# Reordering the end and the start of a scan unit: two masks ahead of the state's update, the first level between the masks, the state product inside the output products

## Chip, core and metric

The kernel runs on one core of one Trainium2 chip. The metric is device time in microseconds (us) of one execution. All arithmetic is fp32.

## What is computed

The reference is a two-layer network on 512 tokens of width 1024 (256 of context, 256 latent). Layer 0 mixes the tokens with a delta-rule scan (RWKV-7) and a diagonal scan, layer 1 with differential attention, and each layer ends in a table of 16384 experts of which every token gathers 128. The change lies in the delta-rule scan alone. It runs forwards and backwards over 8 heads of 64:

```python
def step(state, inp):
    r_t, w_t, k_t, v_t, kk_t, akk_t = inp
    sa = jnp.einsum('bhvk,bhk->bhv', state, kk_t)
    state = (state * w_t[:, :, None, :] - sa[..., None] * akk_t[:, :, None, :]
             + v_t[..., None] * k_t[:, :, None, :])
    return state, jnp.einsum('bhvk,bhk->bhv', state, r_t)
```

## The kernel before

`rwkv_scan` (L620) replaces the 512 steps by blocks of 128 tokens. A *unit* is one block in one direction. There are 8 (`UNITS`, L629), forwards and backwards in turn, and they run one after the other. Inside a unit every head needs four 128 x 128 products of its operands (the *scores*), masked to a triangle, and the inverse of a unit triangular matrix. Lines are those of the kernel before.

- **Scores (`scores`, L744, matmul at L747).** The scores of `bF` with `qrF` go to PSUM banks 6, 7, 4, 5 (`AE_BANKS`), those of `kF` with `qrF` to banks 0 to 3 (`BF_BANKS`). A call makes one pair of heads. Pairs 0 and 1 fill banks 6 and 7 (or 0 and 1), pairs 2 and 3 fill 4 and 5 (or 2 and 3).
- **Masks (L1019).** VectorE multiplies each of these eight banks by the triangle `seen` and writes `NE` (from the bF scores) or `BF` (from the kF scores), four instructions each, counted by the semaphore `seen_done`.
- **Levels.** The inverse `T` is built by doubling, `LEVELS` = 7. Level 0 transposes `NE` on TensorE (L805), and VectorE writes the result into the identity under a mask (L1030). Levels 1 to 5, for each group `g` of four heads, multiply `NE` by `T` (L803) and transpose `T` (L809), ScalarE evicts both (L918, L925), TensorE multiplies the two (L817) and VectorE merges the result into `T` (L1034). Level 6 is a half-sized form of it (L800, L819, L1036).
- **BV product (L783).** `BF` times the values, at the start of level 1, evicted by ScalarE (L906) into `qb`.
- **End of a unit.** L825 makes `W` and `U` from the inverse, evicted by ScalarE (L928) and VectorE (L1045). L834 makes the read-out's factor (bank 2, VectorE L1048). L838 to L840 make the state's transition `GT` and increment `H` (banks 4 and 5), which VectorE evicts in L1051, L1053 and two halves of L1056. L847 is the *state product* `GT` times `S0` (bank 0), to which L1062 adds `H` and which L1063 scales (`s_done`). L853, L855 and L857 are the *output products*, six instructions for each pair of heads, accumulated in bank 1 and evicted by L1067 or L1069 (`o_done`).
- **Preparation of the next unit.** It stands amid the levels: `lora` (L715) in level 1, `sums` (L723) in level 3, and `turn` (L730, L741) in levels 4 to 6, each with its part on ScalarE. GpSimd computes the operands between them (`prepare`, L936 to L974).

Every engine has its instructions in one order, written out by hand, and waits on semaphores. Nothing else sets the order. On TensorE an instruction that waits holds all behind it. In the order before, VectorE first waits until the output products of the unit have ended (L1013), then evicts NE's four masks, BF's four masks, and level 0. TensorE makes all scores, waits for NE's four masks, transposes, and waits for BF's four masks.

Of the kernel before, what the change touches and what calls it, by code (L numbers as in the profile page):

```python
# [18 lines left out]
P = 128  # L19
# [600 lines left out]
def rwkv_scan(nc, a, ident, low, rkv, kk, O, KT, rows_out):  # L620
# [13 lines left out]
    with Phase(nc) as ph:  # L634
# [27 lines left out]
        NE = ph.sb("NE", [P, HEADS, 2, P])  # L662
# [34 lines left out]
        with nc.Block() as block:  # L697
# [10 lines left out]
            def _(pe):  # L708
# [55 lines left out]
                for n, (d, t) in enumerate(UNITS):  # L764
                    b = n % 2
                    if n == 0:
                        scores_ae(n, 0)
                        scores_ae(n, 1)
# [3 lines left out]
                    scores_ae(n, 3)  # L772
                    if n >= 1:
                        pe.wait_ge(s_done, n)
                        pe.wait_ge(r_done, n)
                        pe.wait_ge(o_done, n)
                    for pair in range(4):
                        scores(n, kF, BF_BANKS, bf_mm, pair)
                    for lv in range(LEVELS):
# [5 lines left out]
                        for g in range(2):  # L785

                            if g == 1 and n + 1 < NU:
                                if lv == LORA_AT:
                                    lora(n + 1)
                                if lv == SUMS_AT:  # L790
                                    sums(n + 1)
                                if lv in TURN_AT:
                                    turn(n + 1, TURN_AT[lv])
                            if lv:
                                pe.wait_ge(y_done, 2 * (LEVELS * n + lv - 1) + g + 1)
                            else:
                                pe.wait_ge(seen_done, 8 * n + 4)
                            for h in range(4 * g, 4 * g + 4):
                                if lv == LEVELS - 1:
                                    m = nc.tensor.matmul(ps[into[d], g, cols(h)], NE[from_[d], h, 0, into[d]], T[from_[d], h, from_[d]],  # L800
                                                         start=True, stop=True)
                                elif lv:
                                    m = nc.tensor.matmul(ps[:, g, (h % 4) * P:(h % 4) * P + P], NE[:, h, 0], T[:, h], start=True, stop=True)  # L803
                                else:
                                    m = nc.tensor.transpose(ps[:, 4 + g, (h % 4) * P:(h % 4) * P + P], NE[:, h, 0], ident[:])  # L805
                            m.then_inc(x_mm, 1)
                            if lv:
                                for h in range(4 * g, 4 * g + 4):
                                    m = nc.tensor.transpose(ps[:, 4 + g, (h % 4) * P:(h % 4) * P + P], T[:, h], ident[:])  # L809
                                m.then_inc(tt_mm, 1)  # L810
                        if lv:
                            for g in range(2):
                                pe.wait_ge(x_done, 2 * ((LEVELS - 1) * n + lv - 1) + g + 1)
                                pe.wait_ge(tt_done, 2 * ((LEVELS - 1) * n + lv - 1) + g + 1)
                                for h in range(4 * g, 4 * g + 4):
                                    if lv < LEVELS - 1:
                                        m = nc.tensor.matmul(ps[:, 2 + g, (h % 4) * P:(h % 4) * P + P], TT[:, h], X[:, h], start=True, stop=True)  # L817
                                    else:
                                        m = nc.tensor.matmul(ps[from_[d], 2 + g, cols(h)], X[into[d], h, 0:HD], TT[into[d], h, into[d]],  # L819
                                                             start=True, stop=True)  # L820
                                m.then_inc(y_mm, 1)
# [39 lines left out]
            def _(act):  # L861
# [42 lines left out]
                for n, (d, t) in enumerate(UNITS):  # L904
                    act.wait_ge(bv_mm, n + 1)
                    nc.scalar.activation(qb[:, n % 2, :, 1], ps[:, 6].rearrange("p (h d) -> p h d", h=HEADS), ACT.Copy).then_inc(bv_done, 1)  # L906
                    for lv in range(LEVELS):
                        for g in range(2 if lv else 0):
                            if g == 1 and n + 1 < NU:
                                if lv == LORA_AT:  # L910
                                    lora(n + 1)
# [8 lines left out]
                            else:  # L920
# [5 lines left out]
                                                 ACT.Copy).then_inc(tt_done, 1)  # L926
# [1177 lines left out]
```

## Time and profile before

| | |
|---|---|
| Time, median of 3 runs | 3215.91 us (3214.31 to 3221.04) |
| The profiled execution's own time | 3196.97 us |
| Its span | 3195.2 us |
| The scan's units, 8 of them | from about 318 us to 750 us of the span |
| A unit in the steady part | about 54.6 us |
| TensorE busy over the span | 2642.8 us (83%) |
| VectorE busy over the span | 2107.6 us (66%) |

The profiled execution is one run with the hardware profiler on, and it is not one of the three. A row of the timeline gives start, length, engine, line, operation, output and inputs, shape and count; in square brackets stands how long the engine was idle before it and what released it. Consecutive instructions of one line are merged. An fp32 matmul of 8 heads or tiles shows as 16 entries, a transpose as one each. TensorE's lengths reach past the start of the next row, because matmuls are pipelined: the distance from start to start is what a row costs while the engine is fed.

### The profile page before, as it was taken

The numbers are of one execution on the slowest core, as the hardware profiler recorded it, in microseconds if no ns is written. First come the engines' busy times: TensorE is split into PE (matmuls) and PEld (weight loads), VectorE is DVE, ScalarE is ACT, GpSimd is POOL, SyncE is SP. The second block draws the span as 40 slices with busy tenths as digits, with TensorE's granted clock in tenths as the row PEclk, the third lists the DMA queues.
The fourth block names the chain that finished last, engine by engine and source line by source line (L and its number), as shares of the span: only waits on it lengthen the run. The fifth ranks groups of instructions, "written<-read, shape, count | busy, mean of one in ns | idle before, by whom it ended". The sixth has DMA issues, their size and how long they took to land. (4 is left out here: it accounts for less than half of the span.)

```text
span 3195.2 us, 31178 instructions
## 1 busy us (share of the span) xinstructions
PE 2642.8 (83%) x9164; PEld 1307.3 (41%) x9164; DVE 2107.6 (66%) x4866; ACT 678.7 (21%) x1701; POOL 1077.2 (34%) x927
## 2 busy tenths in 40 slices
PE   4996999996899998777877787776987788887776
PEld 2442888884444443222322232223434444432222
DVE  2236333345477777888888888885575577778887
ACT  1025333332112111111111111112014222111111
POOL 0002323222144444444444444441000233344443
PEclk8997999998999999999999999998998899999999
DMA  5224000003589999999999999997421699999998
GB/s 209 73 99 194 1 1 1 1 1 158 213 345 397 403 402 399 421 420 420 418 421 420 420 415 420 421 420 299 180 69 63 259 420 420 420 419 414 421 420 334
DMA packets 137393, 930.65 MB, mean 291 GB/s; under 512 B 16954, under 2 KB 17978, under 8 KB 32330
## 3 DMA queue, kind: packets, MB, share of 16 engines
q0 software_dynamic: 113664, 822.20, 62.8%
q1 hardware_dynamic: 23636, 107.25, 8.9%
q8 instruction: 53, 0.87, 0.1%
q14 instruction: 40, 0.33, 0.0%
HBM read 928.26 MB, written 1.13 MB: 291 GB/s over the span
## 5 line engine op out<-in xcount | busy, mean ns | idle before, releaser
L1441 PE MATMUL psum<-ring,diag 128*128 128x512 f32 x3072 | 1497.0, 623 | 347.9 <-DVE diag L1560 346.3
L1319 POOL DMA_INDIRECT ring<-in_uv,experts x768 | 913.1, 1189 | 1288.2 <-PE psum L1441 1036.7
L1614 DVE CUSTOM_DVE_ANT_0 ring<-ring,hcur 128x1024 f32<-128x1024 f32 x768 | 941.0, 1225 | 300.0 <-DMA ring<-in_uv,experts 271.8
L1441 PEld LDWEIGHTS psum<-ring,diag 128*128 128x128 f32 x3072 | 558.2, 194 | 1200.1 <-DVE diag L1560 726.1
L1349 ACT ACTIVATE gel<-dots 128x1 f32<-128x1 f32 x768 | 148.5, 201 | 1414.6 <-DVE dots L1614 1413.2
L1560 DVE TENSOR_SCALAR diag<-ident,gel,wcur 128x128 f32<-128x128 f32 x768 | 257.0, 344 | 25.7 <-ACT gel L1349 25.7
L1034 DVE COPY_PREDICATED T<-level,psum 128x512 f32<-128x512 uint32 x80 | 58.7, 733 | 177.6 <-PE psum L817 177.6
L344 PE MATMUL psum<-zT,win_ring 128*128 128x512 f32 x368 | 159.2, 592 | 1.4 <-PEq L90 1.4
L1680 PE MATMUL psum<-wqkv_ring,zT 128*128 128x512 f32 x320 | 139.1, 597 | 1.4 <-PEq L90 1.4
L1420 PE MATMUL psum<-yT,w_q 128*128 128x512 f32 (+1 forms) x256 | 121.1, 576 | 2.5 <-issue 2.5
L344 PEld LDWEIGHTS psum<-zT,win_ring 128*128 128x128 f32 x368 | 69.4, 190 | 86.3 <-issue 86.3
L1680 PEld LDWEIGHTS psum<-wqkv_ring,zT 128*128 128x128 f32 x320 | 61.4, 192 | 78.6 <-issue 78.6
L803 PE MATMUL psum<-T,NE 128*128 128x128 f32 x640 | 85.7, 277 | 0.0
L817 PE MATMUL psum<-X,TT 128*128 128x128 f32 x640 | 84.9, 280 | 0.0
L469 POOL DMA_DIRECT2D yT<-in_b_mod x16 | 8.0, 505 | 227.2 <-POOLq L90 227.2
L803 PEld LDWEIGHTS psum<-T,NE 128*128 128x128 f32 x640 | 78.7, 191 | 6.7 <-issue 6.7
L817 PEld LDWEIGHTS psum<-X,TT 128*128 128x128 f32 x640 | 77.6, 191 | 3.9
L1349 ACT ACT_TABLE_LOAD x60 | 77.0, 1283 | 1.0
L1420 PEld LDWEIGHTS psum<-yT,w_q 128*128 128x128 f32 x256 | 49.4, 193 | 63.0 <-issue 60.9
L1420 PEld LDWEIGHTS psum<-oT,w_q 128*128 128x128 f32 x256 | 48.0, 193 | 49.1 <-issue 46.9
L1690 POOL DMA_DIRECT2D wmod<-in_w_mod x16 | 8.5, 534 | 174.3 <-DVE mod_acc L1720 132.5
L918 ACT ACTIVATE X<-psum 128x512 f32<-128x512 f32 x80 | 47.8, 597 | 83.0 <-PE psum L803 82.2
(368 smaller groups left out, 2702.1 us busy)
## 6 DMA issues: line engine op xcount, KB each, us to landing
wmod<-in_w_mod SPq DMA_DIRECT2D x24, 1024.0 KB, 9.0
w_q<-in_w_q SPq DMA_DIRECT2D x36, 512.0 KB, 7.7
wmod<-in_w_mod POOLq DMA_DIRECT2D x16, 1024.0 KB, 5.5
ring<-in_uv,experts POOLq DMA_INDIRECT x768, 10.5
wqkv_ring<-in_w_qkv SPq DMA_DIRECT2D x6, 2048.0 KB, 10.6
win_ring<-in_w_in SPq DMA_DIRECT2D x23, 512.0 KB, 3.7
wring<-in_w_mod SPq DMA_DIRECT2D x4, 2048.0 KB, 11.6
bc<-modulation_rows SPq DMA_DIRECT2D x14, 512.0 KB, 11.4
```

What stands on the lines that cost most here:

```text
L344: m = nc.tensor.matmul(ps[:, c % BANKS], wring[:, c % RING, k], zT[:, k], start=(k == 0), stop=(k == KD - 1))
L803: m = nc.tensor.matmul(ps[:, g, (h % 4) * P:(h % 4) * P + P], NE[:, h, 0], T[:, h], start=True, stop=True)
L817: m = nc.tensor.matmul(ps[:, 2 + g, (h % 4) * P:(h % 4) * P + P], TT[:, h], X[:, h], start=True, stop=True)
L918: nc.scalar.activation(X[:, 4 * g:4 * g + 4], ps[:, g].rearrange("p (h t) -> p h t", h=4), ACT.Copy).then_inc(x_done, 1)
L1034: nc.vector.copy_predicated(T[:, hs], mask, ps[:, 2 + g].rearrange("p (h t) -> p h t", h=4)).then_inc(y_done, 1)
L1319: nc.gpsimd.indirect_dma_start(ring[:, s % RING], None, uv, bass.IndirectOffsetOnAxis(ap=experts[:, n, j:j + 1], axis=0)).then_inc(row_in[ ...
L1349: nc.scalar.activation(gel[:, j:j + 1], dots[:, j:j + 1], ACT.Gelu_apprx_tanh).then_inc(gelu_done, 1)
L1420: i = nc.tensor.matmul(q_bank(m)[:, cols], w_q[:, m, k], hT[:, k, cols], start=(k == 0), stop=(k == KD - 1))
L1441: m = nc.tensor.matmul(ps[:, c], diag[:, j % DIAGS], ring[:, j % RING, D + 512 * c:D + 512 * c + 512], start=(first and j == 0), stop=(las ...
L1560: nc.vector.tensor_scalar(diag[:, j % DIAGS], ident[:], gel[:, j:j + 1], wcur[:, j:j + 1], ALU.mult, ALU.mult).then_inc(diag_done, 1)
L1614: nc.vector.tensor_tensor_reduce(u, u, hcur[:], 1.0, 0.0, ALU.mult, ALU.add, dots[:, j:j + 1]).then_inc(dot_done, 1)
L1680: m = nc.tensor.matmul(ps[:, i % 8], zT[:, k, t * P:(t + 1) * P], wring[:, c % RING, k], start=(k == 0), stop=(k == KD - 1))
```

## The change

It does these things.

1. `NE` gets two buffers (`NE2`), used by units in turn.
2. On TensorE both pairs of the next unit's bF scores for banks 6 and 7 are issued between L825 and L834; before, one stood there and the other after L840.
3. The state product no longer stands ahead of the output products, but after half of them.
4. VectorE makes the next unit's first two NE masks after the eviction of `H`, ahead of the state's update. The wait for the output products at the start of a unit is gone.
5. Level 0 is taken apart: its transposes go to banks 6 and 7 instead of 4 and 5, the first four ahead of the kF scores (after two masks) and the second four amid them (after four masks). On VectorE the two level 0 merges stand before and after the first BF mask.
6. The BV product moves from the start of level 1 to the middle of it, behind both groups' L803 and L809. `lora` of the next unit moves from ahead of group 1's L803 to between the two groups' L817, on ScalarE to the end of level 1.

The diff, cut to its core:

```diff
-        NE = ph.sb("NE", [P, HEADS, 2, P])
+        NE2 = ph.sb("NE", [P, 2, HEADS, 2, P])
...
                     scores_ae(n, 2)
                     scores_ae(n, 3)
+
+                    def first_turn(g):
+                        pe.wait_ge(seen_done, 8 * n + 2 * g + 2)
+                        for h in range(4 * g, 4 * g + 4):
+                            m = nc.tensor.transpose(ps[:, 6 + g, (h % 4) * P:(h % 4) * P + P], NE[:, h, 0], ident[:])
+                        m.then_inc(x_mm, 1)
+
+                    first_turn(0)
                     if n >= 1:
                         pe.wait_ge(s_done, n)
                         pe.wait_ge(r_done, n)
                         pe.wait_ge(o_done, n)
-                    for pair in range(4):
-                        scores(n, kF, BF_BANKS, bf_mm, pair)
-                    for lv in range(LEVELS):
+                    scores(n, kF, BF_BANKS, bf_mm, 0)
+                    scores(n, kF, BF_BANKS, bf_mm, 1)
+                    first_turn(1)
+                    scores(n, kF, BF_BANKS, bf_mm, 2)
+                    scores(n, kF, BF_BANKS, bf_mm, 3)
+                    for lv in range(1, LEVELS):
+                        for g in range(2):
...
+                            pe.wait_ge(y_done, 2 * (LEVELS * n + lv - 1) + g + 1)
+                            if lv == 1:
+                                pe.wait_ge(seen_done, 8 * n + 5 + g)
...
                         if lv == 1:
                             pe.wait_ge(seen_done, 8 * n + 8)
                             for h in range(HEADS):
...
                         for g in range(2):
+                            if lv == LORA_AT and g == 1 and n + 1 < NU:
+                                lora(n + 1)
...
                     if n + 1 < NU:
                         scores_ae(n + 1, 0)
+                        scores_ae(n + 1, 1)
...
-                    if n + 1 < NU:
-                        scores_ae(n + 1, 1)
                     pe.wait_ge(s0_done, n + 1)
-                    pe.wait_ge(g_done, 2 * n + 1)
-                    for p in range(PAIRS):
-                        m = nc.tensor.matmul(ps[:, 0, p * HD:p * HD + HD], GT[:, p], S0[:, p], start=True, stop=True)
-                    m.then_inc(s_mm, 1)
                     pe.wait_ge(r_done, n + 1)
                     for p in range(PAIRS):
+                        if p == PAIRS // 2:
+                            pe.wait_ge(g_done, 2 * n + 1)
+                            for q in range(PAIRS):
+                                m = nc.tensor.matmul(ps[:, 0, q * HD:q * HD + HD], GT[:, q], S0[:, q], start=True, stop=True)
+                            m.then_inc(s_mm, 1)
...
-                    if n >= 1:
-                        dve.wait_ge(o_mm, n)
...
+                    if n == 0:
+                        masked_ne(0, 0)
+                        masked_ne(0, 1)
+                    masked_ne(n, 2)
+                    masked_ne(n, 3)
                     dve.wait_ge(init_done, n + 1)
-                    dve.wait_ge(seen_done, 8 * n + 8)
-                    for lv in range(LEVELS):
+                    first_level(0)
+                    masked_bf(n, 0)
+                    first_level(1)
+                    for i in range(1, 4):
+                        masked_bf(n, i)
+                    for lv in range(1, LEVELS):
...
                     ins.then_inc(g_done, 1)
+                    if n + 1 < NU:
+                        masked_ne(n + 1, 0)
+                        masked_ne(n + 1, 1)
                     dve.wait_ge(g_done, 2 * n + 2)
                     dve.wait_ge(s_mm, n + 1)
```

`masked_ne` and `masked_bf` wait for the bank's scores and issue the same mask instruction as L1019. `first_level` waits for `x_mm` and issues the same merge as L1030, from bank 6 + g.

How the rows move on the engines. First TensorE at the end of a unit, from the last product of `H` on (L747 are scores, L847 the state product, L853 to L857 the output products of a pair). Before:

```order
L840 MATMUL psum<-WU,bn 128x128
L747 MATMUL psum<-qrF,bF 128x256 x2
L847 MATMUL psum<-S_6,low 128x64 x4
L853 MATMUL psum<-BF,rkv 64x128 x2
L855 MATMUL psum<-NE,WU 64x128 x2
L857 MATMUL psum<-X,S_6 64x128 x2
```

and in the changed kernel, where L856 is the state product and L860 to L864 are the output products:

```order
L848 MATMUL psum<-WU,bn 128x128
L860 MATMUL psum<-BF,rkv 64x128 x2
L862 MATMUL psum<-NE,WU 64x128 x2
L864 MATMUL psum<-X,S_6 64x128 x2
L860 MATMUL psum<-BF,rkv 64x128 x2
L862 MATMUL psum<-NE,WU 64x128 x2
L864 MATMUL psum<-X,S_6 64x128 x2
L856 MATMUL psum<-S_6,low 128x64 x4
```

The scores have left this place, and two pairs of output products now stand ahead of the state product.

Then TensorE at the start of the next unit, from the last scores to level 1 (L805 are the transposes of level 0, L783 is the BV product). Before:

```order
L747 MATMUL psum<-qrF,bF 128x256 x4
L747 MATMUL psum<-qrF,kF 128x256 x8
L805 MATMUL psum<-ident,NE 128x128 x8
L783 MATMUL psum<-rkv,BF 128x64 x8
L803 MATMUL psum<-T,NE 128x128 x4
L809 MATMUL psum<-ident,T 128x128 x4
L715 MATMUL psum<-up,lr 128x512 x2
L803 MATMUL psum<-T,NE 128x128 x4
L809 MATMUL psum<-ident,T 128x128 x4
L817 MATMUL psum<-X,TT 128x128 x8
```

and now, where L778 are the transposes of level 0 and L815 is the BV product:

```order
L747 MATMUL psum<-qrF,bF 128x256 x4
L778 MATMUL psum<-ident,NE 128x128 x4
L747 MATMUL psum<-qrF,kF 128x256 x4
L778 MATMUL psum<-ident,NE 128x128 x4
L747 MATMUL psum<-qrF,kF 128x256 x4
L807 MATMUL psum<-T,NE 128x128 x4
L810 MATMUL psum<-ident,T 128x128 x4
L807 MATMUL psum<-T,NE 128x128 x4
L810 MATMUL psum<-ident,T 128x128 x4
L815 MATMUL psum<-rkv,BF 128x64 x8
L824 MATMUL psum<-X,TT 128x128 x4
L715 MATMUL psum<-up,lr 128x512 x2
L824 MATMUL psum<-X,TT 128x128 x4
```

The transposes stand among the scores, the BV product behind level 1's first products, and `lora` (L715) between the two halves of L824.

Last VectorE from the eviction of `H` over the border of the units. Before:

```order
L1056 COPY low<-psum 64x256 x2
L1062 TENSOR_TENSOR S<-psum,low 128x256
L1063 TENSOR_TENSOR S<-S,ends 128x256
L1067 COPY O<-psum 128x512
L1019 TENSOR_TENSOR NE<-psum,seen 128x2x256 x4
L1019 TENSOR_TENSOR BF<-psum,seen 128x2x256 x4
L1030 COPY_PREDICATED T<-level,psum 128x512 x2
L1034 COPY_PREDICATED T<-level,psum 128x512 x10
```

and now, where L1081 evicts `H`, L1090 and L1091 are the state's update, L1095 the output, L1021 the masks and L1039 the merges of level 0:

```order
L1081 COPY low<-psum 64x256 x2
L1021 TENSOR_TENSOR NE<-psum,seen 128x2x256 x2
L1090 TENSOR_TENSOR S<-psum,low 128x256
L1091 TENSOR_TENSOR S<-S,ends 128x256
L1095 COPY O<-psum 128x512
L1021 TENSOR_TENSOR NE<-psum,seen 128x2x256 x2
L1039 COPY_PREDICATED T<-level,psum 128x512
L1021 TENSOR_TENSOR BF<-psum,seen 128x2x256
L1039 COPY_PREDICATED T<-level,psum 128x512
L1021 TENSOR_TENSOR BF<-psum,seen 128x2x256 x3
L1059 COPY_PREDICATED T<-level,psum 128x512 x10
```

Two NE masks have moved ahead of the state's update, and the merges of level 0 now stand around the first BF mask.

## Rows read from the trace of the kernel before

**Rows 1.** Windows around and in the scan: busy us (x instructions) per engine, granted clock, DMA share, GB/s.

```profile
...
250.00:318.00 68.00, 36.88 (x143) 12.49 (x144) 44.22 (x59) 33.30 (x56) 15.91 (x22) 0.72 0.45 179
...
470.70:525.30 54.60, 51.09 (x441) 44.33 (x440) 19.81 (x32) 18.96 (x36) 15.70 (x14) 1.00 0.00 1
...
689.00:750.00 61.00, 54.23 (x507) 47.36 (x505) 24.81 (x41) 14.59 (x27) 1.04 (x1) 1.00 0.00 1
```

**Rows 2.** Timeline of TensorE around the end of unit 2.

```profile
...
470.68 0.70 PE L747 MATMUL psum<-qrF,bF 64*128 64x256 f32 x4
471.62 1.09 PE L834 MATMUL psum<-NE,WU 128*64 128x128 f32 x16 [0.24 <-DVE WU L1045]
...
475.52 0.70 PE L747 MATMUL psum<-qrF,bF 64*128 64x256 f32 x4
477.19 1.08 PE L847 MATMUL psum<-S,low 128*128 128x64 f32 x8 [0.97 <-DVE low L1053]
478.20 0.44 PE L853 MATMUL psum<-BF,rkv 128*64 128x128 f32 x4
...
481.65 0.44 PE L857 MATMUL psum<-X,S 64*64 64x128 f32 x4
482.01 1.14 PE L747 MATMUL psum<-qrF,bF 64*128 64x256 f32 x8
483.04 2.00 PE L747 MATMUL psum<-qrF,kF 64*128 64x256 f32 x16
485.34 1.09 PE L805 MATMUL psum<-ident,NE 128*128 128x128 f32 x8 [0.30 <-DVE NE L1019]
487.73 2.00 PE L783 MATMUL psum<-rkv,BF 128*128 128x64 f32 x16 [1.30 <-DVE BF L1019]
489.56 1.11 PE L803 MATMUL psum<-T,NE 128*128 128x128 f32 x8
490.51 0.60 PE L809 MATMUL psum<-ident,T 128*128 128x128 f32 x4
490.94 1.88 PE L715 MATMUL psum<-up,lr 128*128 128x512 f32 x4
...
493.99 2.12 PE L817 MATMUL psum<-X,TT 128*128 128x128 f32 x16
495.95 1.08 PE L803 MATMUL psum<-T,NE 128*128 128x128 f32 x8
...
509.13 0.63 PE L741 MATMUL psum<-ident,qt 128*128 128x128 f32 x4
```

**Rows 3.** Timeline of VectorE, same stretch.

```profile
...
470.79 0.69 DVE L1045 COPY WU<-psum 128x512 f32<-128x512 f32 x1 [1.81 <-PE psum L825]
...
476.36 0.69 DVE L1053 TENSOR_TENSOR low<-low,ident 128x512 f32<-128x512 f32 x1
476.96 0.87 DVE L1056 COPY low<-psum 64x256 f32<-64x256 f32 x2
...
482.20 0.69 DVE L1069 TENSOR_TENSOR O<-O,psum 128x512 f32<-128x512 f32 x1 [2.94 <-PE psum L857]
482.81 2.48 DVE L1019 TENSOR_TENSOR NE<-psum,seen 128x512 f32<-128x512 f32 x4
485.20 2.47 DVE L1019 TENSOR_TENSOR BF<-psum,seen 128x512 f32<-128x512 f32 x4
487.76 1.34 DVE L1030 COPY_PREDICATED T<-level,psum 128x512 f32<-128x512 uint32 x2
```

**Rows 4.** Timeline of GpSimd during unit 1.

```profile
...
447.31 1.27 POOL L962 TENSOR_TENSOR na<-na,kk 128x512 f32<-128x512 f32 x1
450.16 1.27 POOL L969 TENSOR_TENSOR qt<-kk,ex 128x512 f32<-128x512 f32 x1 [1.57 <-ACT ex L880]
```

**Rows 5.** Timeline of TensorE ahead of unit 0 and in it.

```profile
...
307.21 3.75 PE L723 MATMUL psum<-lw,tri 128*128 128x512 f32 x4 [2.04 <-POOL lw L942]
...
323.85 2.00 PE L783 MATMUL psum<-rkv,BF 128*128 128x64 f32 x16 [1.29 <-DVE BF L1019]
```

More of the change, by code:

```diff
@@ L776, in _ @@
                         pe.wait_ge(o_done, n)
-                    for pair in range(4):
-                        scores(n, kF, BF_BANKS, bf_mm, pair)
-                    for lv in range(LEVELS):
+                    scores(n, kF, BF_BANKS, bf_mm, 0)
[5 more added lines that the diff above has]
+                        for g in range(2):
+                            if g == 1 and n + 1 < NU:
+                                if lv == SUMS_AT:
+                                    sums(n + 1)
+                                if lv in TURN_AT:
+                                    turn(n + 1, TURN_AT[lv])
+                            pe.wait_ge(y_done, 2 * (LEVELS * n + lv - 1) + g + 1)
+                            if lv == 1:
+                                pe.wait_ge(seen_done, 8 * n + 5 + g)
+                            for h in range(4 * g, 4 * g + 4):
+                                if lv == LEVELS - 1:
+                                    m = nc.tensor.matmul(ps[into[d], g, cols(h)], NE[from_[d], h, 0, into[d]], T[from_[d], h, from_[d]],
+                                                         start=True, stop=True)
+                                else:
+                                    m = nc.tensor.matmul(ps[:, g, (h % 4) * P:(h % 4) * P + P], NE[:, h, 0], T[:, h], start=True, stop=True)
+                            m.then_inc(x_mm, 1)
+                            for h in range(4 * g, 4 * g + 4):
+                                m = nc.tensor.transpose(ps[:, 4 + g, (h % 4) * P:(h % 4) * P + P], T[:, h], ident[:])
+                            m.then_inc(tt_mm, 1)
                         if lv == 1:
@@ L785, in _ @@
                         for g in range(2):
[L787 to L797, printed above, removed]
+                            if lv == LORA_AT and g == 1 and n + 1 < NU:
+                                lora(n + 1)
@@ L798, in _ @@
+                            pe.wait_ge(x_done, 2 * ((LEVELS - 1) * n + lv - 1) + g + 1)
+                            pe.wait_ge(tt_done, 2 * ((LEVELS - 1) * n + lv - 1) + g + 1)
                             for h in range(4 * g, 4 * g + 4):
-                                if lv == LEVELS - 1:
-                                    m = nc.tensor.matmul(ps[into[d], g, cols(h)], NE[from_[d], h, 0, into[d]], T[from_[d], h, from_[d]],
+                                if lv < LEVELS - 1:
+                                    m = nc.tensor.matmul(ps[:, 2 + g, (h % 4) * P:(h % 4) * P + P], TT[:, h], X[:, h], start=True, stop=True)
+                                else:
+                                    m = nc.tensor.matmul(ps[from_[d], 2 + g, cols(h)], X[into[d], h, 0:HD], TT[into[d], h, into[d]],
@@ L801, in _ @@
                                                          start=True, stop=True)
[L802 to L821, printed above, removed]
+                            m.then_inc(y_mm, 1)
@@ L926, in _ @@
                                                  ACT.Copy).then_inc(tt_done, 1)
+                        if lv == 1:
+                            act.wait_ge(bv_mm, n + 1)
+                            nc.scalar.activation(qb[:, n % 2, :, 1], ps[:, 6].rearrange("p (h d) -> p h d", h=HEADS), ACT.Copy).then_inc(bv_done, 1)
+                        if lv == LORA_AT and n + 1 < NU:
+                            lora(n + 1)
                     act.wait_ge(wu_mm, n + 1)
@@ L1009, in _, with masked, masked_ne @@
                 step(nc.vector.tensor_copy(KT[:, t], t1[:]))
+                def masked(dst, bank, n, i):
+                    h = heads_of(i)[0]
+                    nc.vector.tensor_tensor(dst[:, h:h + 3:2].rearrange("p h a t -> p h (a t)"),
+                                            ps[:, bank].rearrange("p (h t) -> p h t", h=2),
+                                            seen[:, UNITS[n][0]].unsqueeze(1).broadcast_to([P, 2, 2 * P]), ALU.mult).then_inc(seen_done, 1)
+                def masked_ne(n, i):
+                    dve.wait_ge(ae_mm, 4 * n + i + 1)
+                    masked(NE2[:, n % 2], AE_BANKS[i], n, i)
@@ L1022, in _, with first_level @@
-                    dve.wait_ge(init_done, n + 1)
-                    dve.wait_ge(seen_done, 8 * n + 8)
-                    for lv in range(LEVELS):
+                    NE = NE2[:, b]
+                    def first_level(g):
+                        dve.wait_ge(x_mm, 2 * LEVELS * n + g + 1)
+                        nc.vector.copy_predicated(T[:, 4 * g:4 * g + 4], level[:, d, 0].unsqueeze(1).broadcast_to([P, 4, P]),
+                                                  ps[:, 6 + g].rearrange("p (h t) -> p h t", h=4)).then_inc(y_done, 1)
```

23 lines of the change are left out of this document (6 added, 17 removed).

## Prediction

> **What bounds the kernel now.** I read the windows first, then TensorE's timeline over one border of units, then VectorE's over the same border, and last GpSimd's preparation of the next unit. The windows show that TensorE is the bound of the scan: in a unit of 54.6 us it is busy for 51.09 us, VectorE for 19.81, ScalarE for 18.96 and GpSimd for 15.70, with next to no DMA [rows 1]. What TensorE does not fill is 3.5 us a unit, and the timeline puts 2.81 us of it into four stops around the border: 0.24 us before L834 (VectorE evicts W and U), 0.97 before the state product L847 (VectorE makes GT in L1051 and L1053), 0.30 before the transposes L805 (NE's masks) and 1.30 before the BV product L783 (BF's masks) [rows 2]. The remaining two stops, in level 6 and before L825, are not touched. VectorE's side of it: after H is evicted by 477.83 us it stands idle until the output products have ended (2.94 us before L1069), and only then makes eight masks and two merges in one go, 482.81 to 489.10 us [rows 3]. So the masks are late for no reason of the arithmetic: two of their four bF score pairs were in PSUM by 476.2 us. From L803 at 489.56 on TensorE has all it needs.
>
> **The price of TensorE's rows when it is fed**, from start to start [rows 2]: two pairs of scores 1.03 us (482.01 to 483.04); the state product 1.01 (477.19 to 478.20); four pairs of output products 3.81 (478.20 to 482.01), so 0.95 a pair; four products of L803 0.95; four transposes 0.43 (490.51 to 490.94); the BV product 1.83 (487.73 to 489.56); eight products of L817 1.96 (493.99 to 495.95); `lora` 1.67 (490.94 to 493.99 less 0.95 and 0.43). A mask or a merge on VectorE follows the last after 0.61 us: 482.81 to 485.20 for four [rows 3]. A release reaches the other engine about 0.14 us after the row ends (L1053 ends at 477.05, L847 starts at 477.19).
>
> **The border, walked again.** I keep the clock of rows 2, from 470.68 on, where L825 is issued.
>
> 1. *Both score pairs ahead of L834.* They take 1.03 us, to 471.71, by the price above. W and U are there at 471.62 [rows 2, 3]. So the second pair fills the stop of 0.24 us and costs 0.09. L834 to L840 move by that: the products of H are issued by 475.61.
> 2. *State product amid the output products.* Two pairs of output products run to 477.51. GT is ready at 477.19, so the stop of 0.97 us is gone. State product to 478.52, two more pairs to 480.43. Before, this was 482.01: 1.58 us earlier. On VectorE the two NE masks follow the eviction of H, 477.83 to 479.1. They delay the state's update (L1062, L1063), which could have begun at about 478.7, to some 480.0. Who waits for it? Only the kF scores, below, at 481.9: hidden with 1.9 us to spare.
> 3. *Scores and level 0.* The last bF scores run to 481.46 and the first four transposes, whose two masks ended at 479.1, to 481.89. The output is evicted from 480.62 to 481.31, in time for the kF scores in banks 0 and 1 (to 482.9). VectorE makes NE's masks 3 and 4 from about 481.4 (the scores are then there) to 482.7, so that the second transposes can be issued at 482.9, with hardly 0.1 us to spare, to 483.3. The other kF scores run to 484.3. The stop of 0.30 us is gone.
> 4. *Level 1.* VectorE merges group 0 (to 483.3), makes BF mask 1 (483.9), merges group 1 (484.5), and makes BF masks 2 to 4 (486.4). TensorE needs the first mask at 484.3, the second at 485.7 and the fourth, for the BV product, at 487.1, after two rounds of 1.38 us. All are there: the stop of 1.30 us is gone. BV to 488.9, L817 and `lora` together 3.63 us, to 492.5. Level 2 starts there, against 495.95 before: **3.4 us a border**. I take 3.3, since the new order changes the kind of matmul three times more, for which no row has a price. The distances where the kind changes are at most 0.1 us longer than within one kind (1.03 for two pairs of scores against 0.95).
>
> The bounds of one border: the idle alone less four such changes, 2.81 - 0.4 = 2.4 us; and the idle with the overhang of the last matmul at each stop, some 0.16 us (L817 lasts 2.12 where 1.96 separate the starts), 2.81 + 4 x 0.16, so 3.5 us. The row of L817 shows that overhang inside a fed stream too, where it costs nothing. The Trainium skill (TensorE: Matmul & The Clock Gate, Single matmul latency) gives a lone warm matmul (398 + N)/2.4 ns where a fed one costs about N/2.4, so each stop that goes away would return 166 ns beyond the idle; by that the border would gain 3.47 us less the changes of kind, and by the idle alone 2.4 to 2.8.
>
> There are seven borders: 7 x 3.3 = 23.1 us. The first unit has no border before it, but its BV product waits 1.29 us for masks [rows 5]. The new order has most of that covered and waits itself for the first two masks, since nothing was masked ahead: 0 to 1.3 us, I take the middle, 0.7. The last unit ends with point 2 alone, 1.0 to 1.7 us, I take 1.6. **Sum: 25.4 us**, between 17.8 (16.8 + 0 + 1.0) and 27.5 (24.5 + 1.3 + 1.7).
>
> *What moves at no cost.* `lora` ends at 491.6 instead of 492.6, 1.0 us earlier where level 2 starts 3.4 us earlier, so GpSimd's chain gains less than TensorE. In unit 1, with the longest chain, L962 ends at 448.58 and L969 begins at 450.16 after waiting 1.57 us for ScalarE's exponentials [rows 4]. With the chain 1.0 us and the exponentials 3.3 us earlier, GpSimd is the later one by 0.7, and L969 ends at 448.9. TensorE transposes `qt` one unit before 509.13, at 454.5 [rows 2], then at 451.2: 2.3 us of cover, and about 1.5 for the operand behind it. ScalarE's eviction of BV (L906) now stands behind level 1's evictions, and `lora`, which reuses its bank, comes half of L817 later, 0.98 us: about as long as the release and one eviction take, so at worst a tenth or two are lost there, inside the bounds. NE's second buffer adds no instruction and no DMA.
>
> Nothing in the scan is bound by a transfer, and the phase behind it starts all its loads after the barrier that ends the scan, so 25 us in the scan are 25 us at the end. Against the profiled execution's own 3196.97 us the sum gives 3171.6. That execution lies 18.9 us below the median of the runs shown, and I forecast the median: 3215.9 - 25.4 = **3190.5 us**. A measurement of this kernel can tell about 0.2% from no change, 6.4 us.
>
> **Rivals.**
>
> *VectorE becomes the bound of the border.* Between the output's eviction and the last BF mask it has nine instructions in a row, and three of its releases have only 0.1 to 0.2 us of room. For it: the 0.1 us at the second transposes. Against it: 0.6 us of room at the BV product. If each hand-over between VectorE and TensorE adds its 0.14 us in turn, level 1 starts about where VectorE lets it, and the border keeps only the 1.6 us of point 2: 8 x 1.6 = 12.8, so 3203. Chance 0.07.
>
> *The clock.* In the scan the granted clock is 1.00, the level of 2.4 GHz, in the stretch ahead it is 0.72 on average, a mix with 1.2 GHz [rows 1], and there four matmuls of 512 columns take 3.75 us instead of 1.88 [rows 2, 5]. A border with another mix of work could make it fall in the scan. Work of x us at the low level costs x us more: at 25.4 us the gain is gone, from 32 us on the kernel is measurably slower; with 7 us in each border and its level 1 it would be 49 - 25 = 24 us slower, 3240. Against it: before, the clock held 1.00 in spite of four stops, and now there are fewer. The Trainium skill (TensorE: Matmul & The Clock Gate, Part 4: PE-mode transpose) says that transposes don't count as busy work for the clock, which speaks for this rival, since the first half of the border holds more of them now; the trace disagrees so far, since levels in which a third of the instructions are transposes ran at 1.00. Chance 0.03.
>
> *It changes nothing that can be told.* If the state product still waits because GT is late, or the preparation chain on GpSimd runs 2 us later than I work out, the levels give the gain back at `turn`. That needs 2.3 us of cover to vanish at each unit and then leaves 0 to 6 us, some 3212. Chance 0.04.
>
> **How the numbers follow.** The forecast has 0.86: 3188 to 3198 by the bounds of the sum. The runs shown lie from 1.6 us below to 5.1 us above their median, which I add below, and above I reach to the first rival's 3203: 3181 to 3203. Faster by over 0.2% are the forecast and the first rival, 0.93; within 0.2% 0.04; slower 0.03.
>
> **What would show it.** In the new profile the state product has no idle before it, the BV product none, level 2 starts some 21.8 us after L825's end instead of 25.3 (495.95 less 470.68), and units repeat after 51.3 us instead of 54.6. The masks after H stand without idle before them, and the state's update ends before 480.5 on this clock. Wrong it would be if idle stands before the second transposes or the BV product of more than 0.3 us, if GpSimd releases the `turn` transposes, or if the scan's clock is below 1.00.

## The result, and the profile after

| | us | runs |
|---|---|---|
| Before, median | 3215.37 (3214.31 to 3221.04) | 4 |
| Changed, median | 3176.23 (3171.08 to 3178.87) | 4 |
| Changed, the profiled execution | 3177.49, span 3175.6 | 1 |

The ratio is 0.9869, with a 95% interval of 0.9857 to 0.9881: 1.3% faster. By the ratio that is some 42 us (38 to 46); the two medians lie 39.1 us apart. The forecast was 3190.5 us, 25.4 us less than before, with a range of 3181 to 3203. The direction was right, but the gain was half as large again as forecast, and the time lies outside the range.

The windows of the changed kernel, whose columns are those of [rows 1]: a unit in the steady part, and unit 0.

```profile
...
318.00:361.00 43.00, 41.28 (x298) 35.73 (x297) 14.77 (x22) 18.37 (x34) 15.02 (x14) 0.88 0.00 1
464.00:516.00 52.00, 51.32 (x448) 44.40 (x447) 19.89 (x33) 19.02 (x36) 15.69 (x14) 1.00 0.01 1
```

TensorE is now busy for 51.3 of 52 us. The border of units 2 and 3, TensorE (L747 are scores, L842 the read-out's factor, L860 the output products, L856 the state product, L778 the transposes of level 0, L815 the BV product, L807 the levels' first products, L741 a part of `turn`):

```profile
...
470.89 1.14 PE L747 MATMUL psum<-qrF,bF 64*128 64x256 f32 x8
471.95 1.09 PE L842 MATMUL psum<-NE,WU 128*64 128x128 f32 x16
...
475.85 0.44 PE L860 MATMUL psum<-BF,rkv 128*64 128x128 f32 x4
...
477.76 1.10 PE L856 MATMUL psum<-S,low 128*128 128x64 f32 x8
...
481.76 0.66 PE L778 MATMUL psum<-ident,NE 128*128 128x128 f32 x4
482.35 1.13 PE L747 MATMUL psum<-qrF,kF 64*128 64x256 f32 x8
483.41 0.66 PE L778 MATMUL psum<-ident,NE 128*128 128x128 f32 x4
484.00 1.13 PE L747 MATMUL psum<-qrF,kF 64*128 64x256 f32 x8
485.06 1.16 PE L807 MATMUL psum<-T,NE 128*128 128x128 f32 x8
...
487.82 1.90 PE L815 MATMUL psum<-rkv,BF 128*128 128x64 f32 x16
...
493.12 1.06 PE L807 MATMUL psum<-T,NE 128*128 128x128 f32 x8
...
506.27 0.63 PE L741 MATMUL psum<-ident,qt 128*128 128x128 f32 x4
```

None of these rows has idle in brackets. In the steady units of this trace TensorE is left with two stops, 0.17 and 0.51 us, both just ahead of the product that makes W and U (L832); the kernel before has them too. The four stops of [rows 2], 0.24, 0.97, 0.30 and 1.30 us, are gone. From the scores ahead of L842 to level 2 it takes 493.12 - 470.89 = 22.23 us, against 25.27 before [rows 2]. VectorE over the same border:

```profile
...
477.29 0.87 DVE L1081 COPY low<-psum 64x256 f32<-64x256 f32 x2
478.20 1.29 DVE L1021 TENSOR_TENSOR NE<-psum,seen 128x512 f32<-128x512 f32 x2
...
479.85 0.42 DVE L1091 TENSOR_TENSOR S<-S,ends 128x256 f32<-128x256 f32 x1
480.89 0.69 DVE L1097 TENSOR_TENSOR O<-O,psum 128x512 f32<-128x512 f32 x1 [0.61 <-PE psum L864]
...
483.07 0.72 DVE L1039 COPY_PREDICATED T<-level,psum 128x512 f32<-128x512 uint32 x1
...
484.89 1.87 DVE L1021 TENSOR_TENSOR BF<-psum,seen 128x512 f32<-128x512 f32 x3
```

The first two masks stand at 478.20, right behind the eviction of H, and the state's update ends at 480.27. BF's last masks end at 486.76, 1.06 us ahead of the BV product. The `turn` of the next unit (506.27 above) has no wait.

The evictions of W and U on VectorE mark the units, one after the other:

```profile
...
419.44 0.69 DVE L1070 COPY WU<-psum 128x512 f32<-128x512 f32 x1 [1.69 <-PE psum L832]
...
470.99 0.69 DVE L1070 COPY WU<-psum 128x512 f32<-128x512 f32 x1 [1.81 <-PE psum L832]
...
522.56 0.69 DVE L1070 COPY WU<-psum 128x512 f32<-128x512 f32 x1 [1.69 <-PE psum L832]
```

A unit takes 51.56 us, against 54.63 in the profiled execution of before (the mean over six units there, from L1045 to L1045): 3.07 us less, where I had forecast 3.3. From the start of the first scores to the start of the last eviction of the output the scan took 410.09 us against 431.64, so 21.6 us less. The two profiled executions differ by 19.5 us as a whole. The timed ones differ by about 40. So the order of work explains about half of what was measured, and the profile that I had argued from does not contain the other half.

### The profile page after: what moved, and what is told of

It reads as the page before. It is cut to its first block and busy times, and to the rows that moved or that the text cites. A ratio compares the mean times of both kernels' runs of the same rounds, so it can differ in the third digit from the quotient of the medians.

```text
span 3175.6 us, 31187 instructions
## 1 busy us (share of the span) xinstructions
PE 2640.8 (83%) x9164; PEld 1303.7 (41%) x9164; DVE 2108.9 (66%) x4866; ACT 679.6 (21%) x1701; POOL 1077.6 (34%) x927
## 5 line engine op out<-in xcount | busy, mean ns | idle before, releaser
L807 PE MATMUL psum<-T,NE 128*128 128x128 f32 x640 | 86.0, 277 | 0.0
L824 PE MATMUL psum<-X,TT 128*128 128x128 f32 x640 | 85.1, 279 | 0.0
L824 PEld LDWEIGHTS psum<-X,TT 128*128 128x128 f32 x640 | 78.1, 191 | 6.5 <-issue 3.3
L807 PEld LDWEIGHTS psum<-T,NE 128*128 128x128 f32 x640 | 78.2, 191 | 6.1 <-issue 3.3
```

## The experiments

Two groups, each on one chip, beside runs of the kernel before of their own. The ratios are to those.

| Run | Median us (range, runs) | Ratio, 95% interval | Unit in its trace, us |
|---|---|---|---|
| Before, group 1 | 3215.93 (3200.47 to 3223.72, 18) | | |
| Before, again | 3216.45 (3196.71 to 3224.03, 12) | 0.9998, 0.9982 to 1.0013 | 57.93 |
| Changed, again | 3175.33 (3171.18 to 3178.04, 5) | 0.9876, 0.9854 to 0.9897 | 51.56 |
| End only | 3194.97 (3189.57 to 3205.93, 7) | 0.9946, 0.9925 to 0.9966 | five 54.76, one 53.12 |
| Start only | 3190.24 (3184.73 to 3194.00, 6) | 0.9922, 0.9902 to 0.9942 | 53.09 |
| Before, group 2 | 3216.08 (3210.62 to 3218.73, 7) | | |
| Before, matmuls in the stop | 3195.58 (3192.39 to 3197.17, 4) | 0.9943, 0.9927 to 0.9960 | 54.63 |
| Before, transposes in the stop | 3196.27 (3193.81 to 3200.18, 4) | 0.9941, 0.9925 to 0.9958 | 54.63 |
| Changed, one stop put back | 3196.28 (3195.03 to 3200.03, 4) | 0.9946, 0.9930 to 0.9963 | 54.63 |
| Changed, clock raised ahead of unit 0 | 3178.50 (3175.89 to 3180.75, 4) | 0.9888, 0.9871 to 0.9904 | 51.56, two of 51.77 and 52.94 |

### The kernel before, again

No edit.

> The kernel before, unchanged, against itself. The scan of the two traces accounts for a gain of 20.7 us (the profiled executions differ by 19.5), the timed runs for some 39. If the other 18 us are a state of the whole execution that the kernel before falls into in most runs (theory A), its runs here lie in two groups about 18 us apart, near 3197 and near 3215. If they are a property of this kernel's code or of the profiled execution alone (theory B), the timed runs are all near 3215 and the profiled one near 3197.

The runs lie in two groups, but very unevenly: of the 30 executions of this group's kernel before and its copy, 28 took 3210.9 to 3224.0 us, and two took 3196.7 and 3200.5. Those two have a mean granted clock of 0.956, as the profiled execution of before had (0.955), the others 0.945 to 0.953. This run's profiled execution, 3223.69 us, is one of the many, and it shows what they do that the one I had read does not. Its windows around the border of units 0 and 1 (columns as in [rows 1]):

```profile
...
376.00:378.00 2.00, 1.70 (x16) 1.30 (x14) 2.00 (x4) 0.00 (x0) 0.00 (x0) 1.00 0.03 8
378.00:380.00 2.00, 0.72 (x7) 0.48 (x5) 1.96 (x4) 0.00 (x0) 0.00 (x0) 1.00 0.00 0
380.00:382.00 2.00, 1.98 (x11) 1.99 (x11) 1.33 (x2) 0.00 (x0) 0.00 (x0) 0.60 0.00 0
382.00:384.00 2.00, 2.00 (x11) 2.00 (x11) 0.00 (x0) 0.58 (x1) 0.00 (x0) 0.50 0.00 0
384.00:386.00 2.00, 2.00 (x11) 2.00 (x11) 0.00 (x0) 0.62 (x2) 0.00 (x0) 0.50 0.00 0
386.00:388.00 2.00, 2.00 (x5) 0.89 (x4) 0.00 (x0) 1.01 (x2) 0.00 (x0) 0.70 0.00 0
```

The granted clock is 1.00 (2.4 GHz) up to the border. Between 378 and 380 us TensorE is busy for only 0.72 of 2 us, and behind that the clock is at 0.50 (1.2 GHz) until 387. What is missing of 1.00 in the last four windows, 2 x (0.40 + 0.50 + 0.50 + 0.30) = 3.4 us, stands for 6.8 us at half the clock. Its timeline over the same place, below the BV product of unit 0 (L805 transposes, L783 BV product, L803 and L809 level 1, L715 `lora`):

```profile
...
325.39 2.00 PE L783 MATMUL psum<-rkv,BF 128*128 128x64 f32 x16 [1.30 <-DVE BF L1019]
...
377.63 1.09 PE L805 MATMUL psum<-ident,NE 128*128 128x128 f32 x8 [0.30 <-DVE NE L1019]
380.02 3.37 PE L783 MATMUL psum<-rkv,BF 128*128 128x64 f32 x16 [1.30 <-DVE BF L1019]
383.18 2.02 PE L803 MATMUL psum<-T,NE 128*128 128x128 f32 x8
384.99 1.06 PE L809 MATMUL psum<-ident,T 128*128 128x128 f32 x4
385.84 2.57 PE L715 MATMUL psum<-up,lr 128*128 128x512 f32 x4
```

The waits are those of [rows 2], 0.30 and 1.30 us, but the work behind them has become slow: BV 3.37 us instead of 2.00, L803 2.02 instead of 1.11. This comes back in all seven borders: the unit takes 57.93 us instead of 54.63, 3.30 us more each, and the scan 454.74 us instead of 431.64. In unit 0, which has no border ahead of it, the same stop of 1.30 us brings no fall: the clock stays at 1.00 behind 325.39 and the BV product takes 2.00 us. Theory A holds for this kernel in the sense that its executions differ in the clock: in this trace it falls at each border, in the first profiled one at none. By their times, 3 of the 42 executions of this kernel that I have, the first profiled one among them, are of the second kind. How many borders fall in each of the other 39 no trace shows. The one profiled here is among the slowest, 7 us above the median of its runs.

### The changed kernel, again

No edit.

> The changed kernel again. Theory A: two groups here too, near 3172 and 3190. Theory B: all runs at 3171 to 3179 and a ratio of 0.987 as before. If the first comparison was only luck of a few runs, the ratio here is 0.992, what the scan's own 25 us give.

It has one group, 3171.18 to 3178.04 us, and no fall of the clock at any border (units of 51.55 to 51.57). The part of theory A that foresaw a slow group here too was wrong. The expectation of a lucky sample falls as well: the interval of the ratio, 0.9854 to 0.9897, leaves out its 0.992. Between the two profiled executions of this group the scan shrinks by 454.74 - 410.06 = 44.7 us.

### The end of a unit alone

```diff
                     if n + 1 < NU:
                         scores_ae(n + 1, 0)
+                        scores_ae(n + 1, 1)
...
-                    if n + 1 < NU:
-                        scores_ae(n + 1, 1)
                     pe.wait_ge(s0_done, n + 1)
-                    pe.wait_ge(g_done, 2 * n + 1)
-                    for p in range(PAIRS):
-                        m = nc.tensor.matmul(ps[:, 0, p * HD:p * HD + HD], GT[:, p], S0[:, p], start=True, stop=True)
-                    m.then_inc(s_mm, 1)
                     pe.wait_ge(r_done, n + 1)
                     for p in range(PAIRS):
+                        if p == PAIRS // 2:
+                            pe.wait_ge(g_done, 2 * n + 1)
+                            for q in range(PAIRS):
+                                m = nc.tensor.matmul(ps[:, 0, q * HD:q * HD + HD], GT[:, q], S0[:, q], start=True, stop=True)
+                            m.then_inc(s_mm, 1)
```

> Only the end of a unit is changed: both score pairs ahead of L834 and the state product after half of the output products. By my walk each of 8 units gives 1.6 us: 12.8 us, ratio 0.996, units of 53.0 us. If the change moved the rest of the kernel into another alignment (theory A), the ratio may lie up to 18 us lower or not at all, whatever the scan gives: 0.990 or 0.996.

The price of the order was right: the one unit whose clock did not fall took 53.12 us, 1.51 less than 54.63, and from the last eviction of W and U to that of the output it took 9.77 us instead of 11.42. The ratio is 0.9946, whose interval still holds the 0.996 expected, but the medians lie 21 us apart. The clock still falls at five of the seven borders, behind the two stops that this kernel keeps, only it comes back sooner. It doesn't fall at the last two. It falls once more in unit 7, at the product of W and U, behind stops of 0.17 and 0.52 us. Windows of its trace at the border of units 0 and 1:

```profile
...
376.00:378.00 2.00, 0.79 (x8) 0.56 (x6) 2.00 (x4) 0.00 (x0) 0.00 (x0) 1.00 0.00 0
378.00:380.00 2.00, 1.91 (x17) 1.91 (x18) 1.38 (x3) 0.00 (x0) 0.00 (x0) 1.00 0.00 0
380.00:382.00 2.00, 2.00 (x11) 2.00 (x11) 0.00 (x0) 0.71 (x2) 0.00 (x0) 0.50 0.00 0
382.00:384.00 2.00, 2.00 (x7) 1.24 (x6) 0.00 (x0) 1.08 (x2) 0.00 (x0) 0.64 0.00 0
384.00:386.00 2.00, 2.00 (x14) 1.52 (x14) 0.00 (x0) 1.42 (x3) 0.43 (x1) 1.00 0.00 0
```

It is low for 3.4 us instead of 6.8, and the fall costs 54.76 - 53.12 = 1.64 us instead of 3.30. So a border gains 1.5 us by the order and as much again by the clock; the scan of this trace takes 428.95 us against 454.74. The stops of 0.24 and 0.97 us that this kernel removes are not needed for the clock to fall. That they have a share in how long it stays low is likely, but no run shows it: two traces are compared here, and the order of the work differs as well.

### The start of a unit alone

The changed kernel with the end of a unit as before; against the changed kernel:

```diff
                         scores_ae(n + 1, 0)
-                        scores_ae(n + 1, 1)
...
+                    if n + 1 < NU:
+                        scores_ae(n + 1, 1)
                     pe.wait_ge(s0_done, n + 1)
+                    pe.wait_ge(g_done, 2 * n + 1)
+                    for p in range(PAIRS):
+                        m = nc.tensor.matmul(ps[:, 0, p * HD:p * HD + HD], GT[:, p], S0[:, p], start=True, stop=True)
+                    m.then_inc(s_mm, 1)
                     pe.wait_ge(r_done, n + 1)
                     for p in range(PAIRS):
-                        if p == PAIRS // 2:
-                            pe.wait_ge(g_done, 2 * n + 1)
-                            for q in range(PAIRS):
-                                m = nc.tensor.matmul(ps[:, 0, q * HD:q * HD + HD], GT[:, q], S0[:, q], start=True, stop=True)
-                            m.then_inc(s_mm, 1)
```

> Only the start of a unit is changed (masks ahead, level 0 between the masks, BV product behind), the end of a unit is as before, with its stop of 0.97 us ahead of the state product. By my walk a border gives 3.3 less 1.6, so 1.7 us: 7 x 1.7 + 0.7 = 12.6 us, ratio 0.996, units of 52.9 us. The two parts should add up to the whole change if nothing else is at work.

A unit takes 53.09 us, 1.54 less than 54.63, so the two parts' orders add up (1.51 + 1.54 = 3.05, the whole has 3.07). The clock of its trace doesn't fall at any of the seven borders, with the stop of 0.97 us still there. The waits of TensorE in this trace (us in total, times, the longest) are

```profile
...
PE psum L854 <- DVE low L1078: 8.4, 8, 1.6
PE psum L832 <- DVE TT L1061: 4.1, 8, 0.5
PE psum L841 <- DVE WU L1070: 2.6, 8, 0.9
```

So that stop, 1.0 us in each of units 0 to 6 (L854 is the state product), did not let the clock fall. In unit 7, where no scores of a next unit fill a part of it, the stop is 1.60 us, and there the clock did fall:

```profile
...
735.18 1.17 PE L854 MATMUL psum<-S,low 128*128 128x64 f32 x8 [1.60 <-DVE low L1078]
...
736.00:738.00 2.00, 2.00 (x17) 1.22 (x16) 0.85 (x2) 0.00 (x0) 0.00 (x0) 0.51 0.00 0
```

The ratio, 0.9922, is below the 0.996 that I expected, which lies outside its interval. The order alone was worth 0.996, and the seven falls at the borders went with the two stops of 0.30 and 1.30 us. This run doesn't tell which of the two mattered; the fillers below take away the longer one alone.

### Fillers in the stop, matmuls and transposes

```diff
                         if lv == 1:
+                            for _ in range(5):
+                                nc.tensor.matmul(ps[:, 7, 0:P], ident[:], ident[:], start=True, stop=True)
                             pe.wait_ge(seen_done, 8 * n + 8)
```

and for the second run ten times `nc.tensor.transpose(ps[:, 7, 0:P], ident[:], ident[:])` at the same place.

> The kernel before, with five more matmuls (128x128x128, identity times identity, into free bank 7) in the stop of 1.30 us ahead of the BV product. By their price of 0.22 us they end before the masks do, so nothing waits for them. In the trace of the kernel before, run again, the granted clock falls to the low level behind this stop in nearly every unit and comes back some 7 us later, which costs 3.3 us a unit. Theory C (the stops let the clock fall, and the change gained 25 us by order and 15 to 18 by the clock): the clock stays at 1.00 in the scan and the time falls to 3197, ratio 0.994, though not one wait is removed. Rival D (the fall has another cause, such as the phase of the program against the clock's controller or the mix of transposes): ratio 1.000, the falls stay.

> The same stop of the kernel before filled with ten transposes of the identity instead, 1.1 us in all. If transposes count as work for the clock as matmuls do, the result is that of the run with five matmuls, 3197. If they don't, the falls stay and the time is 3216.

Both are theory C to within 1.5 us: 3195.58 and 3196.27 us, ratios 0.9943 and 0.9941, against 3196.97 for the one execution of before without falls. The trace with matmuls (L782 the filler, L807 transposes, L785 BV product, L805 level 1):

```profile
...
377.71 1.09 PE L807 MATMUL psum<-ident,NE 128*128 128x128 f32 x8 [0.30 <-DVE NE L1021]
378.64 1.28 PE L782 MATMUL psum<-ident 128*128 128x128 f32 x10
380.11 2.00 PE L785 MATMUL psum<-rkv,BF 128*128 128x64 f32 x16 [0.18 <-DVE BF L1021]
381.94 1.11 PE L805 MATMUL psum<-T,NE 128*128 128x128 f32 x8
```

and that with transposes:

```profile
...
378.81 1.26 PE L782 MATMUL psum<-ident 128*128 128x128 f32 x10
380.27 2.00 PE L785 MATMUL psum<-rkv,BF 128*128 128x64 f32 x16 [0.21 <-DVE BF L1021]
382.11 1.11 PE L805 MATMUL psum<-T,NE 128*128 128x128 f32 x8
```

TensorE still waits for the same masks, and a unit takes 54.63 us in both. Nothing was reordered. What came back, 20 us, is the clock alone: the BV product takes 2.00 us again, and the clock doesn't fall anywhere in the scan of either trace. Both expectations of rival D, a ratio of 1.000 and falls that stay, failed. It also shows that transposes hold the clock as matmuls do here. The Trainium skill (TensorE: Matmul & The Clock Gate, Part 4: PE-mode transpose) says that transpose mode doesn't count as busy work in the same way. The trace disagrees: ten transposes in 1.26 us kept the clock at 1.00 from 340 to 750 us, as five matmuls in 1.28 us did.

### One stop put back

```diff
-                    for i in range(1, 4):
-                        masked_bf(n, i)
+                    masked_bf(n, 1)
+                    dve.wait_ge(seen_done, 8 * n + 6)
+                    for _ in range(3):
+                        step(nc.vector.tensor_tensor(seen[:], seen[:], seen[:], ALU.mult))
+                    masked_bf(n, 2)
+                    masked_bf(n, 3)
```

> The changed kernel, with three useless multiplications on VectorE ahead of the last two BF masks, so that the BV product waits again for some 1.2 us, while all other stops stay away. By the wait alone: 8 x 1.2 = 10 us more than the changed kernel, 3186, the clock at 1.00. If one stop of this length is enough for the clock to fall, 3186 + 7 x 3.3 = 3209. From the run in which only the end was changed, where two stops of 0.30 and 1.30 us stood close together, I expect the second less than the first: a single stop is shorter than the two with four transposes' work between.

Measured was 3196.28 us, 21 us more than the changed kernel: between the two cases, and my leaning to the first was wrong. The stop is 1.14 us long, and in its trace the clock falls at all seven borders:

```profile
...
381.61 0.60 PE L810 MATMUL psum<-ident,T 128*128 128x128 f32 x4
383.35 2.00 PE L815 MATMUL psum<-rkv,BF 128*128 128x64 f32 x16 [1.14 <-DVE BF L1021]
385.19 1.73 PE L824 MATMUL psum<-X,TT 128*128 128x128 f32 x8
386.71 2.98 PE L715 MATMUL psum<-up,lr 128*128 128x512 f32 x4
389.52 1.05 PE L824 MATMUL psum<-X,TT 128*128 128x128 f32 x8
```

L824's first half takes 1.73 us instead of 1.11 and `lora` 2.98 instead of 1.89: the clock falls a little later than in the kernel before, and is low for 3.4 us. A unit takes 54.63 us, 3.07 more than the changed kernel. Of these some 1.7 us are the clock (0.62 at L824, 1.09 at `lora`) and 1.31 the wait: from L810 to the BV product it is 383.35 - 381.61 = 1.74 us, where the changed kernel has 0.43. One stop of 1.1 us at each border was enough, where the one of 1.0 us amid the products of the unit's end was not. The length of the stop doesn't decide alone: 1.30 us in unit 0 of the kernel before brought no fall, and 0.17 and 0.52 us ahead of the product of W and U did in three units of other traces. What else decides stays open.

### The clock raised ahead of unit 0

```diff
+                fill(14)
                 pe.wait_ge(up_in, 16)
                 pe.wait_ge(pre_done, 4)
                 lora(0)
+                fill(10)
                 pe.wait_ge(c_in, 16 * 6)
                 sums(0)
+                fill(6)
                 turn(0, range(4))
+                fill(2)
```

`fill(k)` issues k matmuls of the identity with itself into bank 5.

> The changed kernel, with 32 useless matmuls on TensorE in its waits ahead of unit 0 (14 before the first lora, 10 before sums, 6 before turn, 2 before the scores). In the changed kernel's trace those matmuls ran at the low clock level: lora 3.75 us instead of 1.88, sums 3.56, and the first scores 3.79 instead of 1.83. If the fillers raise the clock ahead of lora, 1.9 + 1.7 + 1.9 us come back: 3170.5 against 3175.5. If they only stand in the way of lora, it is 1 to 2 us slower than the changed kernel.

A miss. `lora` and `sums` did become fast (1.96 us each, from 3.75 and 3.56), but what follows ahead of unit 0 waits for VectorE and GpSimd, and the total is 3178.50 us, 3 us above the changed kernel of the other group and with ratios 0.9888 and 0.9876 whose intervals overlap. The scan of its trace is 2.0 us longer than that of the changed kernel, again (412.09 against 410.06): in units 0 and 4 the clock fell behind the two stops that the changed kernel keeps. Unit 4 (L840 is the product of W and U, 2.05 us where the clock holds):

```profile
...
619.14 3.42 PE L840 MATMUL psum<-qb,TT 128*128 128x128 f32 x16 [0.52 <-DVE TT L1069]
...
620.00:622.00 2.00, 2.00 (x11) 2.00 (x11) 0.00 (x0) 0.00 (x0) 0.00 (x0) 0.50 0.00 0
```

So the order of the changed kernel at the border is no guarantee that the clock holds: this trace has the same border and falls elsewhere. No run beat the changed kernel.

## Why the prediction was wrong

**What held.** That TensorE is the bound of the scan and that nothing downstream takes the gain back. The walk over the border, point by point: the second score pair cost 471.95 - 470.89 - 1.03 = 0.03 us; the state product waits for nothing; the output is evicted 1.64 us earlier in the last unit, counted from the eviction of W and U (1.58 worked out, 1.6 taken); the masks and the state's update hide where I put them; `turn` waits for nothing. The border gave 3.07 us for a forecast of 3.3. The walk itself had come to 3.45, and most of what it lacked is the price of four transposes between scores, start to start 0.59 us (481.76 to 482.35) where I had put 0.43, twice. I had read that a change of kind costs at most 0.1 us, and here it is 0.16. The order alone gave 3.07 us in each of six units, 2.88 in the seventh (48.60 less 45.72 us) and 1.64 at the end, 22.9 us; my sum had 24.7 for these. (One reading in the walk is wrong and changes nothing: 470.68 is where the score pair behind L825 starts, not where L825 is issued.)

**What was mis-sized on the small scale.** Unit 0: I took 0.7 us of gain and it lost 1.4. In the trace of the changed kernel the clock was low over its first scores (0.88 for the window of unit 0, above), and they took 3.79 us instead of 2.00. The wait for the first two masks that I had foreseen is hidden behind that. The low clock there is not shown to come from the change: the kernel before with transposes in the stop has the same 3.79 us for its first scores.

**The step that failed** is the last of the sum: "That execution lies 18.9 us below the median of the runs shown, and I forecast the median: 3215.9 - 25.4". I carried a difference of three times the resolution over as if it were a constant of the measurement. It was the trace of another course of the same program: in the second profiled execution the clock falls at seven borders, 3.30 us each, 23 us in all, and the two runs with fillers got 20 us back on the median of the timed ones. The changed kernel removes the stops behind which it fell, so these 20 us went too: 21.6 + 20 = 42 us, where the ratios give 40 to 42. The sum should have been taken from the time of the execution whose trace I had walked, 3196.97 - 25.4 = 3171.6; the medians measured were 3176.23 and 3175.33.

**The rivals.** None of them took place. The one on the clock had the right mechanism and the wrong sign: I asked whether the clock could begin to fall in the changed kernel, and argued "before, the clock held 1.00 in spite of four stops". By the times, that held for 3 executions of 42. The question to ask was whether it holds in the others. The price in it (work at the low level takes twice the time) was about right: 3.37 us for 2.00 and 2.02 for 1.11 in rows that lie wholly or mostly in it.

**What is shown and what is argued.** Shown: the falls of the profiled executions, their place and price, that filling the stop removes them with no other change, and that putting one stop back brings them back. Argued: that the timed executions, of which only the mean clock is known, fall at the same borders as the profiled one. They may fall at fewer, as the kernel with only its end changed does (five of seven). Their mean clocks and their distance of 10 to 27 us from the two fast ones speak for it, as do the two filler runs. Open: what decides which course an execution takes, and why the same stop brings a fall in one unit or trace and not in another. The program is the same, and the phases ahead of the scan differ by 2 to 4 us between profiled executions (the first `lora` starts at 301.42 us in the trace of before, at 303.43 in that of the same kernel again, and at 305.55 in that of the changed one).

## What to carry to other kernels

Before a sum is made from a trace, compare the profiled execution's own time with the timed runs: if it lies outside their range, as 3196.97 us lay below 3214.31, the trace may be of another course, and the difference is to be found and priced first. On TensorE a stop of a microsecond costs more than its length where the clock falls behind it (here 1.6 to 3.3 us more), so its removal can bring twice what the idle column shows. Where the stop can't be removed, cheap useless work in it, into a free bank, can bring the clock's half of the gain: here 20 us for five instructions in each unit. A mean of the clock over a long window hides such falls: 382 us with one of them still read 1.00.

## What the runs showed of the hardware

- The granted clock fell behind stops of 0.30 and 1.30 us close together (seven of seven borders in one trace, five of seven in another, none in a third), behind a single one of 1.14 us (seven of seven), of 1.60 us (the last unit of the run with only the start changed), and behind 0.17 and 0.52 us (three units in two traces). It did not fall behind one of 1.0 us at another place in seven units, nor behind 1.30 us in unit 0. So neither the length of a stop nor its place decides alone.
- At a border of the kernel before it was low for 6.8 us, which cost 3.30 us; it was low for 3.4 us, at a cost of 1.64, where the stops of 0.24 and 0.97 us earlier in the border were missing.
- The same program fell at every border in one profiled execution, 57.93 us in each of six units, and at none in another, 54.63 us in each.
- Ten transposes in the stop held the clock as well as five matmuls: no fall in either scan, 3196.27 and 3195.58 us.
- Four transposes between scores took 0.59 us from start to start, and 0.43 behind matmuls of level 1.
